# Start-up of a decoder step: x and modulation weights first on SP's queue, parameter tables on ACT's, and the preparation re-ordered

## The reference

```
shift, scale, gate = split(c @ w_mod + b_mod, 3)
h = rmsnorm(x, g) * (1 + scale) + shift
x = x + gate * rmsnorm(sublayer(h), g2)
```

## Time and profile before

| | before |
|---|---|
| time, median of 3 runs | 1652.63 us (1652.54 to 1653.09) |
| time of the profiled execution | 1652.34 us |
| its span | 1650.5 us |
| PE busy | 1527.3 us (93%) |
| DVE / ACT / POOL busy | 788.3 / 615.6 / 193.3 us |
| chain that ended last, by engine | PE 81%, DVE 6%, ACT 5%, DMA 3% |
| first mixer product on PE | 61.81 us after the span's start |

### The profile page before, as it was taken

The page is one execution under the profiler, slowest core; times in us unless marked ns, Lnnn a source line. Parts: engine busy times, 40 slices in busy tenths (PEclk is TensorE's granted clock), DMA queues, the critical chain, the costliest instruction groups (busy, mean ns, idle before and its releaser), DMA issues.

```text
span 1650.5 us, 32825 instructions
## 1 busy us (share of the span) xinstructions
PE 1527.3 (93%) x12481; PEld 1382.5 (84%) x12481; DVE 788.3 (48%) x1379; ACT 615.6 (37%) x1083; POOL 193.3 (12%) x208
## 2 busy tenths in 40 slices
PE   4899999899999999999788999988979999999996
PEld 3689996799999999899657855554959999999995
DVE  2524434666415663452122166666266663266624
ACT  3422334433323332342242366654344432233422
POOL 0011122011101112200002100000210110011120
PEclk8899999899999999989988999999999999999998
DMA  8553237333322333713962011344481333233321
GB/s 292 171 160 101 86 106 276 116 89 89 109 83 85 92 100 103 262 31 107 265 198 62 16 27 27 93 145 122 130 303 52 95 91 114 69 89 89 107 85 57
DMA packets 270473, 193.82 MB, mean 117 GB/s; under 512 B 32772, under 2 KB 236852, under 8 KB 270246
## 3 DMA queue, kind: packets, MB, share of 16 engines
q1 hardware_dynamic: 267761, 184.38, 37.3%
q10 hardware_dynamic: 2628, 8.33, 1.4%
HBM read 186.80 MB, written 10.45 MB: 120 GB/s over the span
## 4 chain that ended last, share of the span: by engine, by line
PE 81%; DVE 6%; ACT 5%; DMA 3%; SPq 2%; issue 2%; ACTq 0%; DVEq 0%
PE pu L783 65%; PE pm L988 2%; ACT Pb L1479 2%; PE pu L1001 2%; PE pu L719 2%; DMA mw_w<-in_mod_w 1%; PE pn L703 1%; DVE x L1686 1%; PE pu L731 1%; PE pu L1012 1%; DVE nt L1685 1%; PE pu L978 1%; DMA w_raw<-in_a_w_in 1%; PE pm L719 1%; PE pn L978 1%
## 5 line engine op out<-in xcount | busy, mean ns | idle before, releaser
L783 PE MATMUL pu<-h_hi,w_hi 128*128 128x260 f32 x2240 | 458.6, 286 | 26.6 <-DVE h_lo L1676 17.1
L783 PE MATMUL pu<-h_lo,w_hi 128*128 128x260 f32 x2240 | 455.1, 285 | 0.0
L783 PE MATMUL pu<-h_hi,w_lo 128*128 128x260 f32 x2240 | 454.9, 285 | 0.0
L783 PEld LDWEIGHTS pu<-h_hi,w_hi 128*128 128x128 f32 x2240 | 349.7, 191 | 33.0 <-issue 18.0
L783 PEld LDWEIGHTS pu<-h_hi,w_lo 128*128 128x128 f32 x2240 | 349.5, 191 | 0.0
L783 PEld LDWEIGHTS pu<-h_lo,w_hi 128*128 128x128 f32 x2240 | 349.3, 191 | 0.0
L1702 DVE TENSOR_TENSOR w_lo<-w_raw,w_hi 128x1024 fp32r<-128x1024 f32 (+1 forms) x164 | 215.7, 1316 | 258.7 <-ACT w_hi L1156 210.7
L1156 ACT ACTIVATE w_hi<-w_raw 128x1024 fp32r<-128x1024 f32 (+1 forms) x158 | 175.9, 1117 | 62.2 <-PE pu L783 62.2
L783 PE MATMUL pu<-act_hi,w_hi 128*128 128x260 f32 x832 | 167.8, 283 | 0.1
L783 PE MATMUL pu<-act_hi,w_lo 128*128 128x260 f32 x832 | 167.5, 283 | 0.0
L783 PE MATMUL pu<-act_lo,w_hi 128*128 128x260 f32 x832 | 167.3, 282 | 0.0
(11 more groups left out here) (317 smaller groups left out, 1594.7 us busy)
## 6 DMA issues: line engine op xcount, KB each, us to landing
w_raw<-in_ffn_w_up SPq DMA_DIRECT2D x88, 512.0 KB, 3.8
mw_z<-in_mod_w SPq DMA_DIRECT2D x14, 2048.0 KB, 13.2
w_raw<-in_ffn_w_down SPq DMA_DIRECT2D x32, 704.0 KB, 4.6
w_raw<-in_a_w_in SPq DMA_DIRECT2D x24, 512.0 KB, 3.8
mw_w<-in_mod_w SPq DMA_DIRECT2D x6, 2048.0 KB, 12.5
mw_h<-in_mod_w SPq DMA_DIRECT2D x4, 2048.0 KB, 11.7
w_raw<-in_w_kv SPq DMA_DIRECT2D x12, 512.0 KB, 3.8
w_raw<-in_a_w_out SPq DMA_DIRECT2D x8, 512.0 KB, 3.7
```

What stands on the lines that cost most here:

```text
L783: last = mm(pu[slot][:, PSO + HALF * c:PSO + HALF * (c + 1)], w[:, k, :], h[:, k, HALF * c:HALF * (c + 1)], start=(k == 0 and w is w_hi[s] ...
```

## The change

SP issues `ident` and `xs` first, then the other constants and at once the modulation weights. The 14 table pieces are issued by ACT, on its own queue, ahead of everything else that ACT does. PE transposes `xs` first and waits for the tables and for the constants only where it needs them; ACT's and DVE's copies follow in that order, and DVE's three small copies from the constants (`tables()`) stand between the x groups and the table groups. `prep_done` is given by the copy of the sample tokens, ahead of the histories, which use `sq` instead of `nt[0]` as scratch; the one-element copy is gone. ACT splits the first two weights before the root, with a one-element square root ahead of it that loads the table; DVE splits off `w_lo` before it inverts the root.

```diff
@@ sync
+            sp.dma_start(ident[:, :], A["c_ident"]).then_inc(S["x_in"], 16)
+            sp.dma_start(xs[:, :, :], A["x_prompt"][0].rearrange("(i p) n -> p i n", p=128)).then_inc(S["x_in"], 16)
+            for t, n in ((line, "c_line"), (srow, "c_srow"), (smask, "c_smask"), (rep, "c_rep"), (blk, "c_blk")):
                 sp.dma_start(t[:, :], A[n]).then_inc(S["consts_in"], 16)
...
-                        sp.dma_start(PR[:, t:t + full, :], src[k:k + 128 * full, :].rearrange("(t p) c -> p t c", p=128))\
...
-                        sp.dma_start(PR[p:p + m, t, :], src[k:k + m, :]).then_inc(S["tables_in"], 16)
...
-            sp.dma_start(xs[:, :, :], A["x_prompt"][0].rearrange("(i p) n -> p i n", p=128)).then_inc(S["x_in"], 16)
@@ tensor
-            pe.wait_ge(S["consts_in"], 16 * 8)
+            pe.wait_ge(S["x_in"], 32)
+            for i in range(4):
+                for kk in range(2):
+                    tr_group([xs[:, i, 128 * k:128 * k + 128] for k in range(4 * kk, 4 * kk + 4)])
             pe.wait_ge(S["tables_in"], 16 * N_TABLES)
             for g in range(5):
                 tr_group([PR[0:valid[t], t, :] for t in range(4 * g, 4 * g + 4)])
...
+            pe.wait_ge(S["consts_in"], 16 * 7)
@@ scalar
+                        act.dma_start(PR[:, t:t + full, :], src[k:k + 128 * full, :].rearrange("(t p) c -> p t c", p=128))\
...
+                        act.dma_start(PR[p:p + m, t, :], src[k:k + m, :]).then_inc(S["tables_in"], 16)
...
             rows(0, 2)
+            split_hi("mix_in", 0, 0, first=True)
+            split_hi("mix_in", 0, 1, first=True)
+            fn(warm[:, :], epst[:, :], ACT.Sqrt)
             root(0)
             rows(2, 4)
             act.wait_ge(S["lines_out"], 16)
-            split_hi("mix_in", 0, 0, first=True)
-            split_hi("mix_in", 0, 1, first=True)
@@ vector
-            ch.link(v.tensor_copy(x[:, :, NP:NT], PTv(R_XS, 64).rearrange("p (b k) -> p k b", k=KT)))
+            v.tensor_copy(x[:, :, NP:NT], PTv(R_XS, 64).rearrange("p (b k) -> p k b", k=KT)).then_inc(S["prep_done"], 1)
...
-            v.tensor_copy(st_z[0:1, 0:1], ones[0:1, 0:1]).then_inc(S["prep_done"], 1)
...
             mods(0, 2)
+            split_lo(0, 0, KT)
+            split_lo(1, 1, KT)
             mean(0)
             mods(2, 4)
             norm_scale(0, 4)
-            split_lo(0, 0, KT)
-            split_lo(1, 1, KT)
```

More of the change, by code:

```diff
@@ L424, in _ @@
         def _(sp):
-            for t, n in ((ident, "c_ident"), (srow, "c_srow"), (smask, "c_smask"), (rep, "c_rep"), (blk, "c_blk"),
-                         (line, "c_line")):
+            sp.dma_start(ident[:, :], A["c_ident"]).then_inc(S["x_in"], 16)
+            sp.dma_start(xs[:, :, :], A["x_prompt"][0].rearrange("(i p) n -> p i n", p=128)).then_inc(S["x_in"], 16)
+            for t, n in ((line, "c_line"), (srow, "c_srow"), (smask, "c_smask"), (rep, "c_rep"), (blk, "c_blk")):
                 sp.dma_start(t[:, :], A[n]).then_inc(S["consts_in"], 16)
@@ L429, in _ @@
             sp.dma_start(pti[:, :], A["page_table"].rearrange("a b -> (a b)").unsqueeze(0)).then_inc(S["consts_in"], 16)
[L430 to L448, removed]
-                        sp.dma_start(PR[:, t:t + full, :], src[k:k + 128 * full, :].rearrange("(t p) c -> p t c", p=128))\
[L450 to L453, removed]
-                        sp.dma_start(PR[p:p + m, t, :], src[k:k + m, :]).then_inc(S["tables_in"], 16)
-                        k += m
-                    n_tab += 1
-            assert n_tab == N_TABLES, n_tab
-            sp.dma_start(xs[:, :, :], A["x_prompt"][0].rearrange("(i p) n -> p i n", p=128)).then_inc(S["x_in"], 16)
             def mod_weights(q):
@@ L1194, in affine @@
                         rows(gates + k // 7, gates + k // 7 + 1)
+            n_tab = 0
+            for row, src in ((R_MODB, A["mod_b"].rearrange("l s (t c) -> (l s t) c", c=128)),
+                             (96, A["kv_mod_b"].rearrange("(t c) -> t c", c=128)),
+                             (R_KVG, A["kv_norm_g"].rearrange("(t c) -> t c", c=128)),
+                             (R_ACB, A["a_conv_b"].rearrange("l (t c) -> (l t) c", c=128)),
+                             (R_NG, A["norm_g"].rearrange("l s (t c) -> (l s t) c", c=128)),
+                             (R_ACW, A["a_conv_w"].rearrange("l j (t c) -> (l j t) c", c=128)),
+                             (R_FCB, A["ffn_conv_b"].rearrange("l (t c) -> (l t) c", c=128)),
+                             (R_FCW, A["ffn_conv_w"].rearrange("l j (t c) -> (l j t) c", c=128)),
+                             (R_STA, A["state_conv_a"].rearrange("l b j (t c) -> (l b j t) c", c=128)),
+                             (R_STF, A["state_ffn_conv"].rearrange("l b j (t c) -> (l b j t) c", c=128)),
+                             (R_C, A["c_prompt"].rearrange("b (t c) -> (b t) c", c=128)),
+                             (R_C + 8, A["c_sample"].rearrange("b (t c) -> (b t) c", c=128)),
+                             (R_XS, A["x_sample"].rearrange("b s (t c) -> (b s t) c", c=128))):
+                n, k = src.shape[0], 0
+                while k < n:
+                    t, p = divmod(row + k, 128)
+                    full = (n - k) // 128 if p == 0 else 0
+                    if full:
+                        act.dma_start(PR[:, t:t + full, :], src[k:k + 128 * full, :].rearrange("(t p) c -> p t c", p=128))\
+                          .then_inc(S["tables_in"], 16)
+                        k += 128 * full
+                    else:
+                        m = min(128 - p, n - k)
+                        act.dma_start(PR[p:p + m, t, :], src[k:k + m, :]).then_inc(S["tables_in"], 16)
+                        k += m
+                    n_tab += 1
+            assert n_tab == N_TABLES, n_tab
             for t in range(0, 13, 2):
@@ L1199, in _ @@
                 bank = banks[t % 4]
-                if t < 5:
+                if t >= 8:
                     col = 0
-                    for tile in range(4 * t, 4 * t + 4):
+                    for tile in range(4 * (t - 8), 4 * (t - 8) + 4):
                         n = valid[tile]
@@ L1206, in _ @@
                 else:
-                    i, kk = divmod(t - 5, 2)
+                    i, kk = divmod(t, 2)
                     last = fn(x[:, 4 * kk:4 * kk + 4, 128 * i:128 * i + 128], bank.rearrange("p (k c) -> p k c", k=4), ACT.Copy)
@@ L1588, in _, with tables @@
             v.memset(tab[32:33, :], 1.0).then_inc(S["tab_set"], 1)
[L1589 to L1594, removed]
+            def tables():
+                dve.wait_ge(S["consts_in"], 16 * 7)
+                dve.wait_ge(S["tab_set"], 1)
+                v.tensor_copy(tabp[:, :].rearrange("t (g q f) -> t g q f", g=2, q=4),
+                              tab[:, :].rearrange("t (g f q) -> t g q f", g=2, f=2))
+                v.tensor_reduce(sel9[:, :], ident[:, :].rearrange("p (j r) -> p r j", j=4)[:, 0:NC9, :], AX.X, ALU.add)
+                v.tensor_copy(tabr[:, :].rearrange("t (b h) -> t b h", b=NS), tab[0:32, :].unsqueeze(1).to_broadcast([32, NS, 16]))
             for t in range(1, 15, 2):
+                if t == 9:
+                    tables()
                 dve.wait_ge(S["tr_done"], t + 1)
                 bank = banks[t % 4]
-                if t < 5:
+                if 8 <= t < 13:
                     col = 0
-                    for tile in range(4 * t, 4 * t + 4):
+                    for tile in range(4 * (t - 8), 4 * (t - 8) + 4):
                         n = valid[tile]
@@ L1605, in _ @@
                         col += n
-                elif t < 13:
-                    i, kk = divmod(t - 5, 2)
+                elif t < 8:
+                    i, kk = divmod(t, 2)
                     last = v.tensor_copy(x[:, 4 * kk:4 * kk + 4, 128 * i:128 * i + 128], bank.rearrange("p (k c) -> p k c", k=4))
@@ L1625, in _ @@
                 history(scf[:, l], PTv(R_STF + 704 * l, 704), PTv(R_FCW + 132 * l, 132), 2 * FT,
-                        nt[0][:, 0:352].rearrange("p (k b) -> p k b", b=NS))
-            v.tensor_copy(st_z[0:1, 0:1], ones[0:1, 0:1]).then_inc(S["prep_done"], 1)
+                        sq[:, 0:352].rearrange("p (k b) -> p k b", b=NS))
             def mods(first, last):
```

## The result

The changed kernel takes 1645.14 us (median of 5 runs, 1644.6 to 1648.16), the kernel before 1652.54 in the same series (5 runs, 1650.53 to 1653.09). The ratio is 0.9959, with a 95% interval of 0.9945 to 0.9972: 6.8 us faster, between 4.6 and 9.1. I had forecast 1641.0, with a range of 1637.0 to 1646.5. The direction and the range held; the size was too large by 4.1 us. The number is that of my rival B, but, as the trace shows, not for B's reason.

What follows compares the result with a forecast made beforehand. The chain to `modulate` was taken to bound the kernel, everything behind shifting as one block. `modulate` at 46.5 against 58.1 gains 11.6 us: 1652.34 - 11.6 = 1640.7, plus 0.3 for the median, 1641.0; range 1637.0 to 1646.5.

Steps and rivals of the forecast that it cites:

- rival B: PE runs at half clock again in the modulation transposes and sum of squares: gain 7.4, time 1645.2 us; chance 0.22.
- Parts 2 to 6: Chain from the tables' landing to `modulate`: T + 11.9 + 1.95 + 7.2 + 6.0, so 46.5 against 58.1.
- T: The time in us at which the tables land for PE, forecast as 19.5, with bounds 13.7 and about 34.
- Part 2: Tables on ACT's queue: issuing is hidden, done by 7.5; queues take turns by packet, so tables land at 19.5.
- Part 1: SP's xs and weights earlier: xs lands about 10.1, weights 7.2 to 7.3 us earlier, weights 1 at 23.5.
- Rival A: Queues share by bytes or better: tables at about 15.5, `modulate` at 42.9, gain 15.2, time 1637.4 us; chance 0.18.
- Parts 4 and 6: prep_done ahead of the histories: first modulation transposes at T + 11.9; splits moved: w_lo's 2.36 us leave the chain.
- Part 5: PE's clock: idling only 1.2 us, it stays full; transposes take 1.95, sum of squares 7.2 instead of 9.72.
- C: SP's queue is served first: tables at 34.2, `modulate` 3 to 7 us later, time about 1657.5 us; chance 0.03.
- D: No change: T between 27.8 and 34, or w_raw late; within 0.2% of 1652.6 us; chance 0.05.

Runs made afterwards that it cites:

- e2: The changed kernel with weights 0, 1 and 2 each loaded as two column halves, so 1 KB packets instead of 2 KB; 1642.82 us.
- e9: The changed kernel with ACT issuing the large table pieces first and the ten small ones after them; 1640.28 us, 0.9931 of the kernel before.
- e1: The changed kernel with the 14 table pieces back on SP's queue, between the small constants and weights 0; 1640.94 us.
- e6: The changed kernel with the largest table piece on SP's queue, behind the small constants and ahead of weights 0; 1641.21 us.
- e3: The kernel before with only the computation re-ordered (prep_done ahead of the histories, splits moved), transfers as before; 1645.60 us.
- e4: The changed kernel with histories ahead of prep_done and splits behind the root again; only transfers and PE's transpose order new; 1657.77 us.
- e7: The kernel before with only the computation re-ordered, plus 24 unused transposes on PE between products 0 and 1; 1644.26 us.

## Why the prediction was right or wrong

- **The formula held, in part by chance.** Parts 2 to 6 gave "modulate starts at T + 27.0". With T = 24.07 that is 51.1; it started at 51.17. Its parts too: product transposes at T + 12.0 (11.9), 1.95 as taken for them, 7.1 for the sum (7.2), 6.0 for the rest. But products 0 and 1 took 5.37 us instead of 3.92, partly at half clock, so product 1 ended at 36.2, where the transposes began, and not 1.2 us ahead of them.
- **The step that failed is T in Part 2**, "the tables land at T = 19.5". Turn by turn per packet was right for 12 to 22 us (e2, and 1,438 to 1,431). Two terms of the count were wrong. The turns did not begin at 2 us: the small pieces, which ACT issues first, moved 115 packets in 4 us, and at 12 us ACT's queue had moved 897 packets, where my count needs about 1,300. And the queue had 2,423 packets, not 2,240. So at 12 us 1,526 were left and not some 900; the difference, about 38 for each engine if they are evenly loaded, is at 0.111 us an estimated 4.3 of the 4.5 us, about 3.0 of it for the late start and 1.3 for the packets that are no rows. e9 confirms the first from the other side.
- **Part 1** expected the weights 7.2 us earlier. Weights 1 landed at 26.1 and not at 23.5. The two queues together moved 3.63 MB in 12 to 22 us, 363 GB/s where I had reckoned with 385 to 389, which is about 0.6 us of it; the rest stays open. SP's issue of weights 1 and of weights 3, and their landings, were:

```profile
5.70 2.11 SPq L438 DMA_DIRECT2D mw_z<-in_mod_w  x1
...
34.27 0.37 SPq L438 DMA_DIRECT2D mw_z<-in_mod_w  x1
```

```profile
mw_z<-in_mod_w SPq DMA_DIRECT2D x1, 2048.0 KB, 20.4
...
mw_z<-in_mod_w SPq DMA_DIRECT2D x1, 2048.0 KB, 8.0
```

  Weights 3 were issued only at 34.27 and landed at 42.3, not at 38.6: their buffer is free only when product 0 is done, and product 0 waits for the tables. I had noted that wait and not followed it. It was no harm here, since product 3 needed them later still. In e1 and e6 late weights 3 do bound product 3, but not through this wait: product 0 was over by 23.1, and SP came to issue them only at 28.30 and 28.12, when its issue of `w_raw` was no longer blocked (in e1 from 17.48 for 10.77 us). They landed at 42.4 and 41.2. Rival A had them at 38.6 and `modulate` at 42.9; the best seen is 45.7.
- **Parts 4 and 6 carried the gain.** e3 has them alone and is as fast as the whole. I had put no number on the halves; had I written the sum for the transfers alone, T + 11.9 with 5.5 us of histories more, it would have given the first transposes at 36.9 with my T, no earlier than the 36.43 of before, and at 41.1 with the T of e4, 23.68, where they started at 40.59.
- **Part 5, the clock**, came out as taken, but not for the reason given. The clock did fall twice, at 20.9 in the wait for the tables and at 31.1 (windows after, clock third from the end):

```profile
20.00:21.00 1.00, 0.00 (x0) 0.00 (x0) 0.00 (x0) 0.00 (x0) 0.00 (x0) 0.94 1.09 364
...
31.00:32.00 1.00, 1.00 (x8) 0.23 (x6) 1.00 (x2) 0.84 (x2) 0.00 (x0) 0.56 1.20 293
34.00:35.00 1.00, 1.00 (x12) 0.36 (x8) 1.00 (x2) 1.00 (x3) 0.00 (x0) 0.74 0.11 29
```

  It had risen again by 34.5, before the transposes. In e3 it fell at 31.7 and rose only at 41.9, within the sum of squares; no run shows what sets that difference, so the full clock of the sum came true by luck. What was slow in the change were products 0 and 1, beside which ACT squared anyway.
- **Rivals.** A, C and D are out. B's condition came true, PE idled 7.80 us and the clock fell, but it was back before the transposes; B's time came true with a full-clock sum, so its mechanism did not; a forecast of 4 us less for that reason would have been right by luck.

## What to carry to other kernels

Before moving transfers to another queue to free the first, count packets and not bytes: two hardware queues here took turns row by row, so many short rows beside a backlog of long ones come last, and on one queue in the right order they come first. A change made of several parts is worth pricing part by part on the chip: here an earlier semaphore and an earlier split gave as much as the whole, and moving the tables to the other queue added nothing that the times can tell until the order of the pieces was turned round (e9) or the largest one went back (e6).

## What was not expected of the hardware

- A queue that begins with small pieces moved 115 packets in 4 us beside the other's 371, and one that begins with large pieces 717 beside 288 (e9). The Trainium skill (DMA: Bandwidth & Descriptors, Queues, rings and completion order) has each DMA engine go round the queues packet by packet. The trace agrees where both queues hold large pieces, 1,438 to 1,431; the early 115 to 371 is not in that rule. The packets of the Trainium skill, in the same section, hold several descriptors, while the packets of this trace are 2.0 KB on average on SP's queue and 0.5 KB on ACT's, about one row each.
- The granted clock also fell while PE was busy. In e9 the sum of squares took 8.95 us; PE was busy in the whole of this window, and none of its gaps since 12.5 us had been longer than 1.05 us:

```profile
32.00:33.00 1.00, 1.00 (x4) 0.82 (x3) 0.00 (x0) 0.00 (x0) 0.00 (x0) 0.59 1.04 268
```

  What PE had done before were products with 32 of the columns and transposes of 9 elements. So idle gaps alone, by which I had argued in Part 5, do not tell when the clock falls.
- In e7 the x transposes took 1.7 us for eight instead of 0.87 until 24.7 us, with a granted clock of 1.00 in the rows. So at the start of this program the column did not show the pace.
